# A routed mixture of experts in one decoder step: the down projection of an expert in two separate halves amid the next expert's matmuls

## What is computed

```python
scores = sigmoid(x @ router_w)                      # 64 experts, 8 chosen per token
for each expert e, with the tokens t that chose it:
    hb = silu(x[t] @ exp_gate[e]) * (x[t] @ exp_up[e])      # 1024 -> 256, twice
    routed[t] += (hb @ exp_down[e]) * gate[t]               # 256 -> 1024
x = layer_norm(ALPHA * x + shared + routed)
```

## Time and profile before

| | us |
|---|---|
| median of 3 runs | 1108.03 |
| lowest and highest | 1101.15, 1108.3 |
| the profiled execution's own time | 1108.3 |
| its span, first to last instruction | 1106.5 |
| TensorE (PE) busy in the span | 1034.3 (93%) |
| DVE, POOL, ACT busy | 707.9, 357.1, 241.6 |

### The profile page before, as it was taken

How to read it: one execution, slowest core, us unless ns; L and a number is a source line. 1 busy time by engine, 2 the same in 40 slices (tenths; PEclk the granted TensorE clock), 3 DMA queues, 4 the chain that set the end, 5 groups by cost and what they waited for, 6 DMA issues and landing times.

```text
span 1106.5 us, 31366 instructions
## 1 busy us (share of the span) xinstructions
PE 1034.3 (93%) x13702; PEld 743.6 (67%) x13703; DVE 707.9 (64%) x1531; ACT 241.6 (22%) x503; POOL 357.1 (32%) x357
## 2 busy tenths in 40 slices
PE   7999999869789999999999999998999999999996
PEld 6877887656654468566766677676777777775762
DVE  0789869799675786954577465555546554654438
ACT  2145512244647221001110011111111111100113
POOL 2000010045400001434444444444444444444510
PEclk9998999889769999999999999999999999999998
DMA  7221222240246528589999999999999999999761
GB/s 222 76 59 39 57 58 82 42 159 4 76 133 233 190 106 353 204 297 374 386 386 380 365 385 390 386 392 382 384 383 391 391 387 389 391 384 384 240 191 78
DMA packets 91927, 282.43 MB, mean 255 GB/s; under 512 B 22494, under 2 KB 49631, under 8 KB 66949
## 3 DMA queue, kind: packets, MB, share of 16 engines
q1 hardware_dynamic: 74685, 243.55, 57.4%
q0 software_dynamic: 16160, 33.62, 12.0%
q10 hardware_dynamic: 944, 3.24, 0.8%
HBM read 260.93 MB, written 35.86 MB: 268 GB/s over the span
## 4 chain that ended last, share of the span: by engine, by line
PE 53%; DMA 11%; DVE 10%; issue 3%; ACT 3%; SPq 0%; POOLq 0%; DVEq 0%; ACTq 0%
PE ph L2397 23%; PE ph L2427 16%; DMA scr_f<-arena,row 10%; PE ph L1555 3%; PE ph L1573 2%; DVE w_exp L176 1%; PE ph L1696 1%; PE pz_late L1596 1%; ACT arena L2437 1%; DMA w_exp<-scr_f 1%; PE ph L1444 1%; DVE w_exp L2642 1%; PE pz_late L1513 1%; PE pst L1468 1%; DVE w_exp L2634 1%
## 5 line engine op out<-in xcount | busy, mean ns | idle before, releaser
L2397 PEld LDWEIGHTS ph<-arena,w_exp 128*64 128x64 f32 x8192 | 343.4, 138 | 60.3 <-issue 54.2
L2397 PE MATMUL ph<-arena,w_exp 128*64 128x96 f32 x8192 | 361.5, 247 | 7.0 <-DVE arena L2381 3.6
L2427 PE MATMUL ph<-w_exp,arena 128*96 128x512 f32 x512 | 235.8, 604 | 13.5 <-ACT arena L2437 11.1
L977 POOL DMA_INDIRECT x_area<-scr_x,piece_row x192 | 198.6, 1034 | 82.6 <-issue 59.0
L2462 POOL DMA_INDIRECT scr_f<-arena,row x62 | 92.0, 1484 | 233.7 <-PE ph L2397 203.2
L2427 PEld LDWEIGHTS ph<-w_exp,arena 128*96 128x96 f32 x512 | 78.7, 163 | 126.0 <-issue 114.6
L2415 DVE TENSOR_TENSOR arena<-arena,ph 128x192 f32<-128x192 f32 x64 | 22.6, 353 | 219.7 <-ACT arena L2408 219.7
L523 PE MATMUL pz<-w_exp 128*128 128x260 f32 x672 | 158.8, 395 | 0.3 <-ACT w_exp L335 0.3
L523 PEld LDWEIGHTS pz<-w_exp 128*128 128x128 f32 x672 | 129.8, 196 | 23.6 <-issue 2.7
L2408 ACT ACTIVATE arena<-ph 128x192 f32<-128x192 f32 x64 | 21.2, 330 | 516.6 <-PE ph L2397 510.1
L2381 DVE STREAM_TRANSPOSE arena<-x_area 128x768 f32<-128x768 f32 x64 | 102.2, 1597 | 32.1 <-DMA x_area<-scr_x,piece_row 32.0
(11 more groups left out here) (387 smaller groups left out, 1049.0 us busy)
## 6 DMA issues: line engine op xcount, KB each, us to landing
w_exp<-in_exp_up_dram SPq DMA_DIRECT2D x64, 1024.0 KB
w_exp<-in_exp_down_dram SPq DMA_DIRECT2D x64, 1024.0 KB
w_exp<-in_exp_gate_dram SPq DMA_DIRECT2D x64, 1024.0 KB
w_exp<-in_w_in_dram SPq DMA_DIRECT2D x22, 512.0 KB, 3.9
w_exp<-in_x_prompt_dram SPq DMA_DIRECT2D x8, 512.0 KB, 5.3
w_exp<-in_w_out_dram SPq DMA_DIRECT2D x2, 2048.0 KB, 11.6
w_exp<-scr_f SPq DMA_DIRECT2D x8, 512.0 KB, 6.5
x_area<-scr_x,piece_row POOLq DMA_INDIRECT x192
```

Of the source, the lines that this page charges most:

```text
L977: nc.gpsimd.indirect_dma_start(m.x_pieces[:, s, r, :], None, m.scr_x1.rearrange("t (q c) -> (t q) c", q=QUADS), bass.IndirectOffsetOnAxis( ...
L2397: last = nc.tensor.matmul(pgu[64 * half:64 * half + 64, s % 2, (2 * part + j) * CAP:(2 * part + j + 1) * CAP], w[job.slot][:, k, f0:P * ha ...
L2427: last = nc.tensor.matmul(pyl[0:CAP, c, :], hid[:, s % 2, j, :], m.expert_down[job.slot][:, j, c * 512:(c + 1) * 512], start=(j == 0), sto ...
```

## The change

`DOWN_AMID` becomes a pair of places, 22 and 44, and `down` gets an argument `parts` with the column halves that it is to do. `gate_up` calls it at each place with one half: half 0 after 22 calls, with the waits for `hid_ready` and `down_loaded`, and half 1 after 44 calls. Each half keeps its own wait for its emptied bank and its own `y_done`. The jobs whose `down` isn't inside a `gate_up` (0 and 61 to 63) do both halves at once as before.

```diff
-    DOWN_AMID = 18
+    DOWN_AMID = (22, 44)
...
                         placed += 1
-                        if amid is not None and placed == DOWN_AMID:
-                            amid()
+                        if amid is not None and placed in DOWN_AMID:
+                            amid(DOWN_AMID.index(placed))
...
-    def down(pe, job):
+    def down(pe, job, parts=(0, 1)):
         q, s = job.q, job.s
-        pe.wait_ge(hid_ready, q + 1)
-        pe.wait_ge(m.down_loaded[job.slot], job.filled)
-        for c in range(2):
+        if 0 in parts:
+            pe.wait_ge(hid_ready, q + 1)
+            pe.wait_ge(m.down_loaded[job.slot], job.filled)
+        for c in parts:
             if job.has_before(1):
                 pe.wait_ge((y_act, y_dve)[c], q)
...
             if amid:
-                gate_up(pe, Job(q + 1), lambda: down(pe, Job(q)))
+                gate_up(pe, Job(q + 1), lambda c: down(pe, Job(q), (c,)))
```

## The result

| | us |
|---|---|
| before, median of 17 runs (lowest, highest) | 1108.3 (1101.15, 1111.85) |
| changed kernel, median of 17 runs (lowest, highest) | 1116.4 (1112.74, 1119.84) |
| ratio, with its 95% interval | 1.0082 (1.0062 to 1.0102) |
| predicted | 1117.8 |
| the profiled execution of the changed kernel (its span) | 1116.72 (1115.0) |

A forecast was written before the change was run, and what follows sets the result against it. TensorE's own instruction stream was taken as the bound, with weights arriving in time. From 1108.3 us, 19.8 added for second visits and 10.3 given back from stalls made 1117.8 us, range 1110 to 1125.

The forecast's parts named there:

- The second visit: On TensorE, entering and leaving `down` once more costs 0.33 us in each of 60 jobs: 19.8 us added.
- What is given back: TensorE stalls shortened by the later first half and the longer period: 10.3 us together.
- waits for ACT's emptying: Sixteen TensorE stalls before `down` until ACT empties its PSUM bank: 7.4 of 11.1 us come back.
- waits before `down` that the view calls issue: Three TensorE waits for which the profile shows no cause: their 0.9 us comes back.
- pieces too short to be listed: Small unlisted TensorE stalls in the stretch, 6.1 us in all: 1.0 us taken as given back.
- the slow `down` of the earlier trace: A `down` at 1008.21 us, 1.7 us too long, partly at the lower clock: left as it is.
- 0.66 us per stall: Cap on each stall's gain before `down`: start 0.33 us later within the period, plus a period 0.33 us longer.
- rival 1: Nothing is given back, since add latency follows the period and stalls before `down` stay: 1128 us; chance 0.14.
- What is queued behind: Behind `down`'s later second half no queue is delayed, and nothing moves past a DMA.
- A free visit: The second visit to `down` costs nothing and 10.3 us come back: 1098 us; chance 0.07.
- rival 2: All TensorE stalls vanish, 17.3 us, as the DMA engines get air; the second visit is paid: 1110.8 us; chance 0.12.
- rival 4: The DMA engines set the pace, stalls and seams only share out the same time: 1108 us; chance 0.05.

The follow-up runs named there:

- `one40`: The kernel before with `down` in one piece after 40 calls of `gate_up` in place of 18: 1090.31 us, ratio 0.9874.
- `wide64_40`: The kernel before with `down` in one piece after 40 calls, as two 64-column tiles with hidden rows padded to 128 columns: 1086.52 us, ratio 0.9809.
- `one22`: The kernel before with `down` in one piece after 22 calls of `gate_up` in place of 18: 1098.07 us, ratio 0.9924.
- `split18_20`: The changed kernel with the halves of `down` after 18 and 20 calls in place of 22 and 44: 1122.44 us, ratio 1.0145 to before.
- `split40_52`: The changed kernel with the halves of `down` after 40 and 52 calls in place of 22 and 44: 1103.15 us, ratio 1.0015 to before.
- `four`: The changed kernel with `down` in four visits of one call each, after 22, 30, 44 and 52 calls: 1150.47 us, ratio 1.0428 to before.
- `tile64_split`: The changed kernel with `down` of jobs 1 to 60 narrowed from 96 to 64 columns, slots 64 to 95 left out: 1087.4 us, ratio 0.9834 to before.

## Why the prediction was right

The time, 1116.4 for 1117.8, and its sign came out.

**What bounds the kernel.** Right. TensorE's stream was the bound, and the DMA engines, full by their share, were not: `one40` shortened the stage by 17.6 us at the same share. `wide64_40` shows how near their bound was, some 8 us further on.

**The second visit, 19.8 us.** Right in size and cause: plain periods 9.36 for 9.37, 0.33 us per visit up to four visits, and nothing in one tiling mode. The seams of the stretch make some 19 us.

**What is given back, 10.3 us.** The sum held: the stretch grew by 10.2 us with 59 seams of 0.32 us in it, 18.9 us, so some 9 came back. Its terms did not, and that their sum held is luck (us, from the two traces; the small pieces are counted as in the prediction, 573.74 less 59 x 9.36, 14 detours of 0.48 and the 13.1 us listed; of the 6.1 before, 1.1 are waits inside `gate_up` that the view does list, as issue):

| term | forecast | before and changed | given back |
|---|---|---|---|
| waits for ACT's emptying | 7.4 | 11.1, 8.3 | 2.8 |
| waits before `down` that the view calls issue | 0.9 | 0.9, 1.2 | -0.3 |
| pieces too short to be listed | 1.0 | 6.1, 1.7 | 4.4 |
| two waits for the transpose | 1.0 | 3.6, 3.6 | 0 |
| the slow `down` of the earlier trace rows | 0 | 1.7, none | 1.7 |
| sum | 10.3 | | 8.6 |

The step that failed is the first. It said that the point of a stall moves by 0.33 us within the period "and the period itself grows by 0.33 us, in which the add goes on: 0.66 us per stall". The first half is borne out: the later place alone gave 8.4 us (`one22`). The second held in part at best: the longer period alone took the waits before `down` only from 12.0 to 11.4 us (`split18_20`). ACT's own waits for adds were 28.4 us in 35 times in the changed kernel, where a fixed latency under periods 0.33 us longer would have cut the 26.1 of the earlier trace rows by up to a third of a microsecond each. The traces show what happened instead: the adds take longer when the period does. From an add's issue to its last update the median of 58 adds is 7.54 us before, 7.46 in `one22` and 7.51 in `one40`; with periods of 9.36 us it is 7.71 in the changed kernel, 7.68 in `split18_20` and 7.62 in `split40_52`; and with 10.02 us, in `four`, it is 8.11. So the add eats a third to two thirds of what the period adds. One execution of each kernel can't say how sure that is, but all four kernels with longer periods go the same way, and `tile64_split`, with two visits and periods of 8.71 us, has 7.46. That is the mechanism of rival 1 in part; the whole of that rival (1128) didn't come. Why the adds slow down was not tried. The forecast of 4 us or less for the waits on ACT was wrong accordingly (8.3). One execution's list of waits is one draw, so such terms carry several microseconds of chance: the medians say 8.4 for the place and 16 for the split, and these are firmer than any of the single terms.

**What is queued behind.** Right: in the changed kernel, `split40_52` and `four`, with pieces as late as 52 calls, no later piece of `down` waited for its bank or its weights; all waits stand before the first.

**The rivals.** A free visit was refuted by every pair of runs that changes width, and the pair of one width has it (8.71 us with one visit and with two). All stalls gone and the seam paid, rival 2, is what `split40_52` built: a ratio of 1.0015 (0.999 to 1.004), where the 1110.8 of that rival is 1.0023 times 1108.3. The changed kernel itself kept 8.3 us of stalls for ACT. The DMA engines as the pace, rival 4, holds only for kernels faster than any that was compared then.

## What to carry to other kernels

Before a block of matmuls is cut and spread, look at the tile widths on both sides of the cut: between different widths each visit has a price (0.33 us here), paid in all jobs, while the slack that it brings helps only those jobs that stall. What a late operand needs is a later place, which costs nothing: one number, 18 to 40, was worth 1.3%, and a later place in two pieces was worth nothing. Take a stall's cover from the place alone, and don't count on a longer period to give a DMA all of that time when the DMA engines are full. And when two traces are compared, look at the granted clock in both: one fall of 3.41 us to half the clock is worth five visits.

## What the runs showed of the hardware

- Between matmuls of a 64-column and of a 96-column tile, the loader idles 0.79 us and TensorE loses some 0.16 us on each side; between tiles of one width, padded if need be, the loader idles 0.26 us and TensorE loses nothing.
- Two tiles of 64 columns side by side, each streaming 512 columns, take 3.43 us for 16 instructions, as long as 8 instructions on one tile.
- Rows of an indirect add whose numbers lie outside the table are counted in the page's HBM bytes (8.1 MB more with 32 such rows in each of 62 adds) but hardly move anything: the queue had 1984 packets and 0.02 MB more. They are not free: the adds took 8.4 us for 7.5, and the kernel with them took 33 us longer than the one that leaves them out (1119.98 and 1086.52; 41 by the ratios).
- Beside full DMA engines an indirect add's latency is not fixed: its median was 7.5 us with periods of 9.04 us, 7.6 to 7.7 with 9.36, and 8.1 with 10.02.
- The granted clock fell to half for 3.41 us behind some waits of TensorE of 2.0 to 2.4 us, once in the stretch of the kernel before and three times in that of `split18_20`; a wait of 2.2 us in the changed kernel and one of 2.8 us in `one40` passed without it.
